# Attention in an fp32 encoder: weights times values by fp32r products of split halves for half of the key blocks, and GpSimd joins half of the two softmax maps

## The chip, the cores and the metric

The kernel runs on one core of one Trainium2 chip. The metric is the device time of one execution in microseconds. Three executions of the kernel before gave 3018.87, 3022.2 and 3027.47 us, median 3022.2 us.

## The reference

A trunk of two layers, in fp32, on two requests that share the weights: a long one of 2048 tokens ("prompt") and a short one of 256 ("sample"). The first layer is differential attention with 8 heads, the second mixes tokens with a Fourier transform. What matters here is the attention of one head:

```python
s = jnp.einsum('bhmqd,bhmkd->bhmqk', qb, k) * scale        # two maps, m = 0, 1
s = s - (slopes[:, None, None] * dist)[None, :, None]
p = jax.nn.softmax(s, axis=-1)
pd = p[:, :, 0] - lam * p[:, :, 1]
return jnp.einsum('bhqk,bhkv->bhqv', pd, v)
```

There are 16 blocks of 128 query rows and 16 blocks of 128 keys in the prompt; a value row has 128 elements. The sample has two blocks of each.

## The kernel before

The program is a sequence of stages on one core: a projection (tiles `ia_`), attention (`pa_`), an output projection (`oa_`), a gate (`fg_`), the Fourier stage (`fl_`) and a last projection (`of_`). In all but the attention's score and value products, a product of fp32 precision is already written as three fp32r products: each operand is split in a high and a low fp32r part, and high by high, low by high and high by low are added up (lines 206 to 208). Only the attention stage (`attend`) changes.

`attend` walks over 8 heads, and in each head over 17 steps `q`: 16 blocks of query rows and one step (`SAMPLE`, q = 16) for the sample. Steps overlap: in step q the scores of block q are made, block q-1 is joined, and block q-2 is transposed (`turned_block`). The order of the work within a step is written by hand in the function `step` of each engine, and each engine runs its list in order.

- **PE** makes the scores of a block in four halves of 1024 columns (`score_half`, lines 1051 to 1055; halves 0 and 1 belong to the first map, 2 and 3 to the second; one of a map's halves has a small diagonal product more, line 1054). A half goes into one of three slots (`RING`) of the PSUM tile `score`, and waits until ACT has taken the half three before it: half 1 of a step waits for exponential 2 of the step before, half 3 for exponential 0 of its own step. Between the halves stand `turn(c)`, four transpositions of 128x128 of the joined weights into the only PSUM tile `turned` (`turn_weights`, line 1083, c = 0 to 3), and `pair(n)`, two key blocks of weights times values (`pair_product`, line 1114). A product of 128x256 is for two query blocks at once, so half of the 16 key blocks come in one step (keys 0 to 7, "part 0") and the rest in the next ("part 1"). In steps 1 to 5 of a head `turn_value` also transposes the head's values.
- **ACT** copies `turned` to SBUF (`take_weights`, line 1181; `take_v`, line 1187), and computes the exponentials (line 1201). Its order is take 0, take 1, exponential 0, take 2, exponential 1, take 3, exponential 2, (values), exponential 3.
- **DVE** takes the maximum of each half (`maximum`, line 1267), turns two of them into the bias of the exponentials (`negative`, line 1273), inverts the row sums (line 1294), and joins the maps: `combine` (line 1305) computes p0 / sum0 + p1 in one instruction of 128x2048.
- **POOL** (GpSimd) scales the second map by -lambda / sum1 first (line 1358, 128x2048).

PE's order of one step before:

```python
half(0); half(1); turn(0); pair(0); turn(1); half(2); pair(1)
turn(2); half(3); turn(3); pair(2); turn_value(q - 1); pair(3)
```

Steps 6 to 15 of a head have all of this and no values to transpose; the prediction calls them, and step 0, plain steps. In step 3 `pair` has only the sample's product, in step 16 the score halves are the sample's, two and short.

## Time and profile before

| | |
|---|---|
| median of three executions | 3022.2 us (3018.87 to 3027.47) |
| the profiled execution's own time | 3030.89 us |
| its span, first to last instruction | 3029.0 us |
| TensorE clock granted, mean over the span | 0.973 |
| busy share of the span, PE / DVE / ACT / POOL | 94% / 64% / 58% / 37% |
| share of the 16 DMA engines, queue q1 | 40.1% |

The profiled execution took 8.7 us (0.3%) more than the median. The shares are means over stages of different kinds. The attention stage lasts from 817 to 2113 us of the span, eight heads of some 159 us each. Matmuls are pipelined and the ends of their rows are modelled, so the step from one start to the next says more of PE than a duration does.

### The profile page before, as it was taken

What the parts mean: (1) busy time and instruction counts of PE and PEld (TensorE: products, weight loads), DVE (VectorE), ACT (ScalarE), POOL (GpSimd) and SP (SyncE); (2) the same over time, 40 slices, a digit from 0 to 9 for tenths busy, and PEclk for the clock granted to TensorE, in tenths of its full rate; (3) what the DMA queues carried; (4) which work ended last, traced back from release to release, by engine and by line L of the source; (5) the groups of instructions that cost most, each with busy time, mean ns of one, the idle gap of its engine ahead of it and who ended that gap; (6) DMA issues with size and microseconds to landing.
All of it is one profiled execution on the core that took longest, in us unless ns stands there. A gap on an engine that the chain in (4) does not pass through costs nothing. (4 is left out here: it accounts for less than half of the span.)

```text
span 3029.0 us, 43689 instructions
## 1 busy us (share of the span) xinstructions
PE 2849.5 (94%) x15098; PEld 2495.8 (82%) x15098; DVE 1945.9 (64%) x2402; ACT 1744.5 (58%) x3126; POOL 1134.4 (37%) x676
## 2 busy tenths in 40 slices
PE   3889999999899999999999999998899899899899
PEld 3889998999878787878787878887688899887687
DVE  7668867866478787878787878787886200351322
ACT  4667766776477777767777777775443321221321
POOL 5887764654222222212222222222664221130642
PEclk8999999999999999999999999999899999999899
DMA  2555454457345414132223232021664622565752
GB/s 84 181 169 165 147 184 133 126 179 194 114 102 164 104 32 105 36 81 63 70 65 78 63 79 64 29 89 33 219 206 153 212 89 76 145 181 180 264 180 105
DMA packets 281842, 374.29 MB, mean 124 GB/s; under 512 B 22923, under 2 KB 258507, under 8 KB 276140
## 3 DMA queue, kind: packets, MB, share of 16 engines
q1 hardware_dynamic: 279404, 369.14, 40.1%
q8 instruction: 127, 2.08, 0.3%
q10 hardware_dynamic: 2080, 2.10, 0.2%
q14 instruction: 103, 0.84, 0.1%
q0 software_dynamic: 128, 0.13, 0.0%
HBM read 258.04 MB, written 125.97 MB: 127 GB/s over the span
## 5 line engine op out<-in xcount | busy, mean ns | idle before, releaser
L1267 DVE TENSOR_REDUCE pa_half_max<-pa_score 128x1 f32<-128x1024 f32 x512 | 625.7, 1222 | 234.8 <-PE pa_score L1055 233.9
L1358 POOL TENSOR_SCALAR pa_p<-pa_p,pa_inv_sum,pa_lam_neg 128x2048 f32<-128x2048 f32 x128 | 263.3, 2057 | 946.3 <-DVE pa_inv_sum L1294 946.3
L1201 ACT ACTIVATE pa_p<-pa_score,pa_neg_max 128x1024 f32<-128x1024 f32 x512 | 568.3, 1112 | 76.2 <-DVE pa_neg_max L1273 72.9
L206 PE MATMUL ia_acc<-ia_xh,ia_wh 128*128 128x384 f32 x1344 | 461.1, 343 | 82.4 <-DVE ia_xl L686 44.2
L1114 PE MATMUL pa_o_acc<-pa_wt,pa_vv 128*128 128x256 f32 x2048 | 511.4, 380 | 1.0 <-ACT pa_o_out_s L1236 0.3
L1051 PE MATMUL pa_score<-pa_ka,pa_qa 128*128 128x512 f32 x1024 | 456.7, 446 | 20.2 <-ACT pa_p L1201 9.2
L207 PE MATMUL ia_acc<-ia_xl,ia_wh 128*128 128x384 f32 x1344 | 457.2, 340 | 0.0
L208 PE MATMUL ia_acc<-ia_xh,ia_wl 128*128 128x384 f32 x1344 | 456.8, 340 | 0.0
L1181 ACT ACTIVATE pa_wt<-pa_turned 128x512 f32<-128x512 f32 x512 | 306.5, 599 | 260.8 <-PE pa_turned L1083 260.4
L1055 PE MATMUL pa_score<-pa_kb,pa_qb 96*128 96x512 f32 x1024 | 424.1, 414 | 0.0
L1114 PEld LDWEIGHTS pa_o_acc<-pa_wt,pa_vv 128*128 128x128 f32 x2048 | 367.3, 190 | 44.9 <-ACT pa_o_out_s L1236 2.1
L443 POOL TENSOR_TENSOR ia_w_sums<-ia_raw 128x512 f32<-128x512 f32 x240 | 334.7, 1402 | 178.5 <-PE ia_acc L208 156.3
L206 PEld LDWEIGHTS ia_acc<-ia_xh,ia_wh 128*128 128x128 f32 x1344 | 258.8, 193 | 89.3 <-issue 89.1
L1083 PE MATMUL pa_turned<-pa_ident,pa_p 128*128 128x128 f32 x2048 | 314.7, 276 | 10.4 <-ACT pa_wt L1181 9.6
L1083 PEld LDWEIGHTS pa_turned<-pa_ident,pa_p 128*128 128x128 f32 x2048 | 238.8, 140 | 90.6 <-ACT pa_wt L1181 49.5
L1305 DVE SCALAR_TENSOR_TENSOR pa_p<-pa_p,pa_inv_sum 128x2048 f32<-128x2048 f32 x128 | 300.3, 2346 | 0.1
L670 DVE TENSOR_TENSOR ia_wl<-ia_acc,ia_wh 128x512 fp32r<-128x512 f32 x336 | 227.7, 684 | 95.8 <-ACT ia_acc L569 94.5
L706 DVE TENSOR_TENSOR ia_c<-ia_c,ia_acc 128x384 f32<-128x384 f32 x384 | 198.6, 548 | 126.5 <-PE ia_acc L208 116.7
L207 PEld LDWEIGHTS ia_acc<-ia_xl,ia_wh 128*128 128x128 f32 x1344 | 259.0, 193 | 0.9 <-issue 0.6
L208 PEld LDWEIGHTS ia_acc<-ia_xh,ia_wl 128*128 128x128 f32 x1344 | 258.6, 192 | 0.0
L1051 PEld LDWEIGHTS pa_score<-pa_ka,pa_qa 128*128 128x128 f32 x1024 | 196.7, 192 | 65.7 <-ACT pa_p L1201 21.2
L1055 PEld LDWEIGHTS pa_score<-pa_kb,pa_qb 96*128 96x128 f32 x1024 | 197.3, 193 | 33.3
(281 smaller groups left out, 4843.4 us busy)
## 6 DMA issues: line engine op xcount, KB each, us to landing
ia_raw<-attn_w_in SPq DMA_DIRECT2D x46, 1024.0 KB, 6.7
qk_hi<-ia_hi SPq DMA_DIRECT2D x96, 192.0 KB, 3.4
qk_lo<-ia_c SPq DMA_DIRECT2D x96, 192.0 KB, 3.2
pa_ka<-qk_hi SPq DMA_DIRECT2D x32, 512.0 KB, 6.6
fl_slices<-normed SPq DMA_DIRECT2D x26, 512.0 KB, 6.6
ia_h<-x_cols SPq DMA_DIRECT2D x24, 384.0 KB, 6.4
v<-ia_c SPq DMA_DIRECT2D x48, 192.0 KB, 5.8
attn_gate<-ia_c SPq DMA_DIRECT2D x48, 192.0 KB, 1.9
```

The costliest lines, as they stand in the source:

```text
L206: pe.matmul(out, a_hi(k), b_hi(k), start=first and n == 0, stop=False)
L207: pe.matmul(out, a_hi(k), b_lo(k), start=False, stop=False)
L208: mm = pe.matmul(out, a_lo(k), b_hi(k), start=False, stop=last and n == len(ks) - 1)
L443: pool.tensor_tensor(w_sums[:, s % RING], x, y, op).then_inc(w_sum, 1)
L1051: pe.matmul(out[:, c], qa[s][:, n, at:at + P], ka[hs][:, n, cols], start=True, stop=False)
L1055: mm = pe.matmul(out[:, c], qb[s][:, n, at:at + P], kb[hs][n][:, cols], start=False, stop=True)
L1083: mm = pe.transpose(turned[:, x * P:(x + 1) * P], src, ident[:])
L1114: mm = pe.matmul(o_acc[:], vv[:, k], wt[:, g % 2, k], start=k == 0, stop=k == NB - 1)
L1181: act.activation(wt[:, s, 4 * c:4 * c + 4, at:at + P], turned[:].rearrange("p (k t) -> p k t", k=4), ACT.Copy).then_inc(turned_out, 1)
L1201: act.activation(dst[:, half * HALF:(half + 1) * HALF], score[:, (4 * q + j) % RING].rearrange("p a b -> p (a b)"), ACT.Exp, bias=neg_max[ ...
L1267: dve.tensor_reduce(half_max[:, q % 2, n, half:half + 1], score[:, (4 * q + j) % RING].rearrange("p a b -> p (a b)"), AX_X, ALU.max).then_ ...
L1305: dve.scalar_tensor_tensor(out=a, in0=a, scalar=inv_sum[:, par, 0:1], in1=p1[:, par], op0=ALU.mult, op1=ALU.add).then_inc(weights, 1)
```

## The change

Key blocks 4 to 11 (`LOW = (1, 2)`, the transposition groups c = 1 and 2) are held as two fp32r tiles each instead of one of fp32. ACT's copy of `turned` writes the high part (`wt_hi`, `vv_hi`), DVE then subtracts it from `turned` and writes the low part (`weights_low`, `v_low`). PE's product of such a block is three fp32r matmuls of 128x256 in place of the fp32 one. A transposition that follows group 1 or 2 now waits, besides for ACT's copy, for DVE's subtraction (`low_out`). In PE's order pair(2) stands ahead of turn(3), and pair(3) ahead of the values.

Joining the maps is divided: DVE's `combine` and GpSimd's first scaling cover keys 0 to 1023; for keys 1024 to 2047 GpSimd does it all, with two scalings and an addition of 128x1024 (`weights_rest`), for which turn(2) and exponential 3 wait. Tiles are laid out anew to make room: the sample's diagonal table is dropped (one DMA of 64 KB less in each head), and the lambda vectors and the squares of the tail lie where other tiles lie at other times.

```diff
     SHORT, T0 = S_SAMPLE, S_PROMPT
+    LOW = (1, 2)
+    LOW_NB = 4 * len(LOW)
     SCORES = 4 * NB + 2
...
-        vv = m.sb("vv", [P, NB + 2, P])
+        vv = m.sb("vv", [P, NB + 2 - LOW_NB, P])
+        vv_hi = m.sb("vv_hi", [P, LOW_NB, P], F32R)
+        vv_lo = m.sb("vv_lo", [P, LOW_NB, P], F32R)
-        wt = m.sb("wt", [P, 2, NB, PAIR])
+        wt = m.sb("wt", [P, 2, NB - LOW_NB, PAIR])
+        wt_hi = m.sb("wt_hi", [P, 2, LOW_NB, PAIR], F32R)
+        wt_lo = m.sb("wt_lo", [P, 2, LOW_NB, PAIR], F32R)
...
-        weights = m.sem("weights")
+        weights, weights_rest = m.sem("weights"), m.sem("weights_rest")
...
                 def turn_weights(h, t, c):
+                    b = turned_block(t)
                     if c == 0:
                         pe.wait_ge(weights, STEPS * h + t - 1)
+                    if c == 2:
+                        pe.wait_ge(weights_rest, NB * h + t - 1 if t >= 2 else NB * h)
                     wait(pe, turned_out, unit(h, t, "w", c))
-                    b = turned_block(t)
+                    wait(pe, low_out, lows(h, t, "w", c))
                     for x in range(4):
                         if b == SAMPLE:
...
                         pe.wait_ge(turned_out, unit(h, NC, "v", NC - 1) + 1)
+                        pe.wait_ge(low_out, lows(h, 1 + LOW[-1], "v", LOW[-1]) + 1)
                     for k in range(k0, k0 + 2):
-                        mm = pe.matmul(o_acc[:], vv[:, k], wt[:, g % 2, k], start=k == 0, stop=k == NB - 1)
+                        if not is_low(k):
+                            mm = pe.matmul(o_acc[:], vv[:, full_at(k)], wt[:, g % 2, full_at(k)], start=k == 0, stop=k == NB - 1)
+                            continue
+                        at = low_at(k)
+                        pe.matmul(o_acc[:], vv_hi[:, at], wt_hi[:, g % 2, at], start=False, stop=False)
+                        pe.matmul(o_acc[:], vv_hi[:, at], wt_lo[:, g % 2, at], start=False, stop=False)
+                        pe.matmul(o_acc[:], vv_lo[:, at], wt_hi[:, g % 2, at], start=False, stop=False)
                     if k0 == NB - 2:
                         mm.then_inc(pair_done, 1)
 
...
                     turn(2)
                     half(3)
+                    pair(2)
                     turn(3)
-                    pair(2)
+                    pair(3)
                     turn_value(q - 1)
-                    pair(3)
...
                     s, at = (b // 2) % 2, (b % 2) * P
-                    act.activation(wt[:, s, 4 * c:4 * c + 4, at:at + P], turned[:].rearrange("p (k t) -> p k t", k=4),
-                                   ACT.Copy).then_inc(turned_out, 1)
+                    dst = wt_hi[:, s, low_at(4 * c):low_at(4 * c) + 4, at:at + P] if c in LOW else \
+                        wt[:, s, full_at(4 * c):full_at(4 * c) + 4, at:at + P]
+                    act.activation(dst, turned[:].rearrange("p (k t) -> p k t", k=4), ACT.Copy).then_inc(turned_out, 1)
 
                 def take_v(h, t, c):
                     act.wait_ge(turns, unit(h, t, "v", c) + 1)
                     n = 4 if c < NC else 2
-                    act.activation(vv[:, 4 * c:4 * c + n], turned[:, :n * P].rearrange("p (k t) -> p k t", k=n),
-                                   ACT.Copy).then_inc(turned_out, 1)
+                    dst = vv_hi[:, low_at(4 * c):low_at(4 * c) + n] if c in LOW else vv[:, full_at(4 * c):full_at(4 * c) + n]
+                    act.activation(dst, turned[:, :n * P].rearrange("p (k t) -> p k t", k=n), ACT.Copy).then_inc(turned_out, 1)
 
...
                         act.wait_ge(weights, STEPS * h + q - (1 if q >= 2 else 2))
+                    if j == 3 and not (is_first(h) and q < 2):
+                        act.wait_ge(weights_rest, NB * h + (q - 1 if q >= 1 else -1))
...
-                    a, par = p0[:, (q - 1) % 4], (q - 1) % 2
-                    dve.scalar_tensor_tensor(out=a, in0=a, scalar=inv_sum[:, par, 0:1], in1=p1[:, par],
+                    a, par = p0[:, (q - 1) % 4, :HALF], (q - 1) % 2
+                    dve.scalar_tensor_tensor(out=a, in0=a, scalar=inv_sum[:, par, 0:1], in1=p1[:, par, :HALF],
                                              op0=ALU.mult, op1=ALU.add).then_inc(weights, 1)
+
+                def weights_low(h, t, c):
+                    dve.wait_ge(turned_out, unit(h, t, "w", c) + 1)
+                    b = turned_block(t)
+                    s, at = (b // 2) % 2, (b % 2) * P
+                    ks = slice(low_at(4 * c), low_at(4 * c) + 4)
+                    dve.tensor_tensor(wt_lo[:, s, ks, at:at + P], turned[:].rearrange("p (k t) -> p k t", k=4),
+                                      f32(wt_hi[:, s, ks, at:at + P]), ALU.subtract).then_inc(low_out, 1)
+
+                def v_low(h, t, c):
+                    dve.wait_ge(turned_out, unit(h, t, "v", c) + 1)
+                    ks = slice(low_at(4 * c), low_at(4 * c) + 4)
+                    dve.tensor_tensor(vv_lo[:, ks], turned[:].rearrange("p (k t) -> p k t", k=4),
+                                      f32(vv_hi[:, ks]), ALU.subtract).then_inc(low_out, 1)
 
                 def step(h, hs, q):
                     parts = step_parts(h, q)
+
+                    def low(c):
+                        if parts["weights"] and (q, "w", c) in place:
+                            weights_low(h, q, c)
                     if q == SAMPLE:
                         maximum_sample(h, 0)
                         inverse_sums(h, q)
                         maximum_sample(h, 1)
+                        low(1)
+                        low(2)
                     else:
                         if parts["score"]:
                             maximum(h, q, 0)
@@ -1319,11 +1381,17 @@
                         if parts["score"]:
                             maximum(h, q, 1)
                             negative(h, q, 0)
+                        low(1)
+                        if parts["score"]:
                             maximum(h, q, 2)
+                        low(2)
+                        if parts["score"]:
                             maximum(h, q, 3)
                             negative(h, q, 1)
                     if parts["before"]:
                         combine(h, q)
+                    if parts["score"] and (q, "v", q - 1) in place and q - 1 in LOW:
+                        v_low(h, q, q - 1)
                 dve.memset(ones[:], 1.0).then_inc(tail_set, 1)
                 dve.memset(eps[:], SUBLN_EPS).then_inc(tail_set, 1)
...
+                    pool.tensor_scalar(p1[:, par, HALF:], p1[:, par, HALF:], inv_sum[:, par, 1:2], lam["neg"][:, 0:1],
+                                       ALU.mult, ALU.mult).then_inc(p1_rest, 1)
+                    pool.tensor_scalar(b, b, inv_sum[:, par, 0:1], ones[:, 0:1], ALU.mult, ALU.mult).then_inc(p0_rest, 1)
+                    hold(pool, pool_rest, p1_rest, NB * h + q)
+                    hold(pool, pool_rest, p0_rest, NB * h + q)
+                    pool.tensor_tensor(b, b, p1[:, par, HALF:], ALU.add).then_inc(weights_rest, 1)
                     if is_last(h) and q == 13:
                         pool.wait_ge(unit_in, 48)
                         for n in range(2):
```

On PE, a plain step of part 0 in the attention stage, from half 2's product pair on. Before (L1114 is an fp32 product of a pair, L1083 the transpositions, L1051, L1054 and L1055 the scores):

```order
L1114 MATMUL pa_o_acc<-pa_wt,pa_vv 128x256 x2
L1083 MATMUL pa_turned<-pa_ident,pa_p 128x128 x4
L1051 MATMUL pa_score<-pa_ka,pa_qa_51 128x512
L1055 MATMUL pa_score<-pa_kb,pa_qb_52 128x512
L1051 MATMUL pa_score<-pa_ka,pa_qa_51 128x512
L1054 MATMUL pa_score<-pa_diag_53,pa_ident_r 128x128
L1055 MATMUL pa_score<-pa_kb,pa_qb_52 128x512
L1083 MATMUL pa_turned<-pa_ident,pa_p 128x128 x4
L1114 MATMUL pa_o_acc<-pa_wt,pa_vv 128x256 x4
```

Now (L1148 is the fp32 product, L1151 to L1153 the three fp32r ones, L1113 the transpositions, L1078 and L1082 the scores):

```order
L1148 MATMUL pa_o_acc<-pa_wt,pa_vv 128x256 x2
L1113 MATMUL pa_turned<-pa_ident,pa_p 128x128 x4
L1078 MATMUL pa_score<-pa_ka,pa_qa 128x512
L1082 MATMUL pa_score<-pa_kb,pa_qb 128x512
L1078 MATMUL pa_score<-pa_ka,pa_qa 128x512
L1082 MATMUL pa_score<-pa_kb,pa_qb 128x512
L1151 MATMUL pa_o_acc<-pa_wt_hi,pa_vv_hi 128x256
L1152 MATMUL pa_o_acc<-pa_wt_lo,pa_vv_hi 128x256
L1153 MATMUL pa_o_acc<-pa_wt_hi,pa_vv_lo 128x256
L1151 MATMUL pa_o_acc<-pa_wt_hi,pa_vv_hi 128x256
L1152 MATMUL pa_o_acc<-pa_wt_lo,pa_vv_hi 128x256
L1153 MATMUL pa_o_acc<-pa_wt_hi,pa_vv_lo 128x256
```

Pair(2), now six matmuls of fp32r instead of two of fp32, has moved in front of the last transpositions.

On DVE, a plain step from the first bias on. Before (L1267 maximum, L1273 bias, L1305 join):

```order
L1273 TENSOR_SCALAR pa_neg_max<-pa_half_max 128x1
L1266 REGISTER_ALU
L1267 TENSOR_REDUCE pa_half_max<-pa_score 128x1
L1266 REGISTER_ALU
L1267 TENSOR_REDUCE pa_half_max<-pa_score 128x1
L1273 TENSOR_SCALAR pa_neg_max<-pa_half_max 128x1
L1297 REGISTER_ALU
L1305 SCALAR_TENSOR_TENSOR pa_p<-pa_p,pa_inv_sum 128x2048
```

Now (L1309 maximum, L1315 bias, L1355 the low parts, L1347 join):

```order
L1315 TENSOR_SCALAR pa_neg_max<-pa_half_max 128x1
L1351 REGISTER_ALU
L1355 TENSOR_TENSOR pa_wt_lo<-pa_turned,pa_wt_hi 128x4x128
L1308 REGISTER_ALU
L1309 TENSOR_REDUCE pa_half_max<-pa_score 128x1
L1351 REGISTER_ALU
L1355 TENSOR_TENSOR pa_wt_lo<-pa_turned,pa_wt_hi 128x4x128
L1308 REGISTER_ALU
L1309 TENSOR_REDUCE pa_half_max<-pa_score 128x1
L1315 TENSOR_SCALAR pa_neg_max<-pa_half_max 128x1
L1339 REGISTER_ALU
L1347 SCALAR_TENSOR_TENSOR pa_p<-pa_p,pa_inv_sum 128x1024
```

A low part now stands ahead of the third and another ahead of the fourth maximum, and the join is half as wide.

## Rows read from the trace of the kernel before

**Rows 1.** Attention stage: us, busy PE, PEld, DVE, ACT, POOL, then clock, DMA share, GB/s.
```profile
817.00:2113.00 1296.00, 1258.38 (x6712) 1031.78 (x6712) 1031.40 (x1221) 938.01 (x1725) 280.51 (x151) 0.99 0.28 75
```

**Rows 2.** PE in order of time, a plain step: start us, duration us, instruction.
```profile
...
1543.58 0.58 PE L1051 MATMUL pa_score<-pa_ka,pa_qa 128*128 128x512 f32 x1
...
1544.71 0.39 PE L1051 MATMUL pa_score<-pa_ka,pa_qa 128*128 128x512 f32 x1
...
1545.76 0.60 PE L1083 MATMUL pa_turned<-pa_ident,pa_p 128*128 128x128 f32 x4
...
1547.06 0.64 PE L1083 MATMUL pa_turned<-pa_ident,pa_p 128*128 128x128 f32 x4
1547.45 0.48 PE L1051 MATMUL pa_score<-pa_ka,pa_qa 128*128 128x512 f32 x1
...
1548.48 1.03 PE L1114 MATMUL pa_o_acc<-pa_wt,pa_vv 128*128 128x256 f32 x4
1549.35 0.60 PE L1083 MATMUL pa_turned<-pa_ident,pa_p 128*128 128x128 f32 x4
1549.70 0.48 PE L1051 MATMUL pa_score<-pa_ka,pa_qa 128*128 128x512 f32 x1
...
1550.84 0.60 PE L1083 MATMUL pa_turned<-pa_ident,pa_p 128*128 128x128 f32 x4
1551.27 1.89 PE L1114 MATMUL pa_o_acc<-pa_wt,pa_vv 128*128 128x256 f32 x8
...
1552.82 0.58 PE L1051 MATMUL pa_score<-pa_ka,pa_qa 128*128 128x512 f32 x1
```

**Rows 3.** DVE in order of time, same step.
```profile
1551.04 1.23 DVE L1267 TENSOR_REDUCE pa_half_max<-pa_score 128x1 f32<-128x1024 f32 x1 [1.13 <-PE pa_score L1055]
1552.30 0.21 DVE L1273 TENSOR_SCALAR pa_neg_max<-pa_half_max 128x1 f32<-128x1 f32 x1
1552.43 2.34 DVE L1305 SCALAR_TENSOR_TENSOR pa_p<-pa_p,pa_inv_sum 128x2048 f32<-128x2048 f32 x1
```

**Rows 4.** ACT in order of time, same step.
```profile
1548.38 1.11 ACT L1201 ACTIVATE pa_p<-pa_score,pa_neg_max 128x1024 f32<-128x1024 f32 x1
...
1549.98 0.60 ACT L1181 ACTIVATE pa_wt<-pa_turned 128x512 f32<-128x512 f32 x1 [0.40 <-PE pa_turned L1083]
...
1552.55 1.12 ACT L1201 ACTIVATE pa_p<-pa_score,pa_neg_max 128x1024 f32<-128x1024 f32 x1 [0.38 <-DVE pa_neg_max L1273]
```

**Rows 5.** All engines in order of time, where a score half waits for ACT.
```profile
1495.72 1.12 ACT L1201 ACTIVATE pa_p<-pa_score,pa_neg_max 128x1024 f32<-128x1024 f32 x1 [0.47 <-DVE pa_neg_max L1273]
...
1496.98 0.19 PEld L1051 LDWEIGHTS pa_score<-pa_ka,pa_qa 128*128 128x128 f32 x1 [0.28 <-ACT pa_p L1201]
1496.98 0.50 PE L1051 MATMUL pa_score<-pa_ka,pa_qa 128*128 128x512 f32 x1
...
1498.08 0.65 PE L1083 MATMUL pa_turned<-pa_ident,pa_p 128*128 128x128 f32 x4
```

**Rows 6.** PE in order of time, fp32r products of 260 columns, Fourier stage.
```profile
2659.77 0.29 PE L206 MATMUL fl_ps<-fl_wc,fl_ring 128*128 128x260 f32 x1
...
2662.41 0.29 PE L207 MATMUL fl_ps<-fl_wc,fl_ring 128*128 128x260 f32 x1
```

**Rows 7.** DVE groups by line: a split's low part, two SBUF inputs beside GpSimd.
```profile
L670 DVE TENSOR_TENSOR ia_wl<-ia_acc,ia_wh 128x512 fp32r<-128x512 f32 x336 | 227.7, 684 | 95.8 <-ACT ia_acc L569 94.5
...
L1780 DVE TENSOR_TENSOR oa_wl<-oa_raw,oa_wh 128x1024 fp32r<-128x1024 f32 x4 | 11.8, 2983 | 8.7 <-ACT oa_wh L1715 8.7
```

**Rows 8.** POOL in order of time, the step's scaling of the second map.
```profile
1547.14 2.05 POOL L1358 TENSOR_SCALAR pa_p<-pa_p,pa_inv_sum,pa_lam_neg 128x2048 f32<-128x2048 f32 x1 [7.16 <-DVE pa_inv_sum L1294]
```

**Rows 9.** POOL groups by line: adding two tiles of 128x1024.
```profile
L1579 POOL TENSOR_TENSOR oa_g_more<-oa_b_more,oa_g_more 128x1024 f32<-128x1024 f32 x8 | 19.2, 2396 | 22.0 <-DVE oa_b_more L1789 22.0
```

**Rows 10.** PE in order of time, the step that scores the short request.
```profile
1455.85 0.64 PE L1083 MATMUL pa_turned<-pa_ident,pa_p 128*128 128x128 f32 x4
...
1457.23 0.66 PE L1083 MATMUL pa_turned<-pa_ident,pa_p 128*128 128x128 f32 x4 [0.75 <-ACT pa_wt L1181]
```

51 lines of the change are left out of this document (35 added, 16 removed).

## The prediction

> **What bounds the kernel now.** I read four views in this order: the busy time of the stage, one plain step engine by engine in order of time, the places where PE stands still, and the groups by line for the prices of what is new. In the attention stage PE is busy 1258 of 1296 us, DVE 1031, ACT 938, POOL 281, at 0.99 of the full clock, the 2.4 GHz level [rows 1]. So PE looks like the bound. The question is whether a shorter product shortens a step, and for that the step has to be walked through.
>
> I count from the start of turn(0), 1545.76 [rows 2]. The next one stands as far after the next half 0 (1552.82) as this one after 1543.58, 2.18 us, so at +9.24: **a plain step takes 9.24 us**. Within it turn(1) starts at +1.30, half 2 at +1.69, pair(1) at +2.72, turn(2) at +3.59, half 3 at +3.94, turn(3) at +5.08, pair(2) and pair(3) from +5.51, next half 0 at +7.06, half 1 at +8.19 [rows 2]. Three chains run beside PE, and the reader should see how little slack they have:
> - *Round trip of `turned`.* ACT begins its copy 0.63 after turn(2) starts (1549.98) and needs 0.60 [rows 4]; with 0.06 to PE that is 1.30 in all, just the distance of turn(0) and turn(1). No slack.
> - *Exponential 0 to half 3.* It starts at +2.62, behind take 1 [rows 4]. A half that waits for an exponential starts 1.26 after the exponential's start (1495.72 to 1496.98) [rows 5]. So half 3 could start at +3.88; it does at +3.94. Slack 0.06.
> - *Half 3 to the next half 1.* Half 3 gives the fourth maximum at +5.28, the bias at +6.54 [rows 3], exponential 2 at +6.79 [rows 4], half 1 possible at +8.05; it starts at +8.19. Slack 0.14.
>
> **The change, part by part.**
>
> *Products on PE.* A pair of fp32 blocks takes 0.87 (1548.48 to 1549.35) [rows 2], 0.434 per block. The nearest fp32r product is one of 260 columns, 0.120 from start to start (22 intervals in 2.64 us) [rows 6]; three make 0.36, and a low pair takes 0.71 instead of 0.87. The bounds for one product are 0.107 (256 columns at 2.4 GHz) and 0.145, at which three cost what the fp32 form does. I take 0.119. Eight heads by eight query pairs by eight low blocks are 512 blocks, so PE is spared some 0.08 x 512 = 41 us. The Trainium skill, "TensorE: Matmul & The Clock Gate", section "Back-to-back issue gap", gives N/2.4 + 2.5 ns, 109 ns for 256 columns; by it PE would be spared 54 us; the trace is 9 ns slower at 260 columns than that formula.
>
> *Low parts on DVE.* The nearest row is the same operation on the same shape, 0.684 [rows 7], and that stage's GpSimd is busy too, so I add nothing for it. DVE starts it 0.04 after ACT's end, as ACT starts after DVE's bias [rows 3, 4]; an instruction that depends on nothing starts 0.08 before the modelled end of the one ahead, as the join does [rows 3]. Two of them cost 1.37 in a step; the join of half the width gives back some 1.07 of its 2.34 [rows 3]. DVE's total is no bound (8 of 9.2 us). Their place is what matters: the second stands ahead of the fourth maximum.
>
> *A step of part 0* (pair 1 full, pairs 2 and 3 low). turn(2) at +3.59 as before; take 2 from +4.22 to +4.82; low part +4.86 to +5.55; fourth maximum at +5.47, where it was +5.28. All behind it moves by 0.19: exponential 2 at +6.98, half 1 at +8.24, while PE by itself would be there at +7.87. The next turn(0), 1.05 later, is at **+9.29**. PE's 0.32 is spent on waiting, and 0.05 more.
>
> *A step of part 1* (pairs 0 and 1 low). turn(1) stays at +1.30, since the round trip holds it: pair(0)'s 0.16 is gone. pair(1) brings turn(2) to +3.43 (its own round trip with the low part, 1.30 + 0.04 + 0.68 = 2.02 after turn(1), allows +3.32). Half 3 is then held by exponential 0 until +3.88. Half 3 and the full pair(2) (1.14 + 0.87), which stands in front now, put turn(3) at +5.89, where it was +5.08; take 3 runs from +6.52 to +7.12, and exponential 2, behind it on ACT, starts at +7.05. Half 1 at +8.31, next turn(0) at **+9.36**; PE alone would allow +9.08.
>
> *What a wait adds.* The half that waited in [rows 5] takes 1.10 without a diagonal product, where half 1 took 1.05 with it (1544.71 to 1545.76) [rows 2]: its weights cannot be loaded early. That is 0.05 and the diagonal product (128 columns at 2.4 GHz, 0.05), 0.10 in all. A wait shorter than a weight load costs less and one that disturbs what follows costs more, so the bounds are 0 and 0.16; I take 0.08. With it a plain step takes (9.29 + 9.36)/2 + 0.08 = 9.40, 0.16 more than now. Ten such steps and step 0, eight heads: 88 x 0.16 = **+14 us**.
>
> *The other steps.* In step 16 no half 2 or 3 hides the round trips, turn(2) to turn(3) is 1.38 already [rows 10], and both gain a subtraction (0.68 + 0.04 each), against which pair(2) now stands between them: +0.4 per head. In step 3 the pairs 1 to 3 are missing: two subtractions, partly hidden by the wait that half 3 has there anyway, +0.2. Steps 1, 2 and 5, in which the values' transposition makes PE's path longer than the chains, keep some 0.12 each: -0.35. Together +0.25 x 8 = **+2 us**. Bounds: nothing and +8.
>
> *Costs of nothing.* GpSimd does three scalings of half of 2.05 [rows 8] and an addition of 2.40 [rows 9], 5.5 us, instead of 2.05; it has 7.16 idle us in front of each scaling [rows 8], and turn(2) and exponential 3 want the result in the next step only. If that cover went, its excess would count in every step. The extra waits before exponential 3 and turn(2) are met long before. The dropped table of the short request is one DMA per head off a queue that nobody waits for here.
>
> The **sum** is +16 us: 3030.9 (the profiled execution, span 3029.0) becomes 3047; against the median, from which the profiled one stands 8.7 us off, **3038 us**. I call a difference under 0.3% (9 us) no change; the three executions differ by as much. Own bounds: 88 times 0.08 for the wait either way and 0.05 of reading error give 3026 to 3050.
>
> **The rivals.**
> 1. *PE's saving arrives.* The chains have more slack than the rows show, for instance because exponentials and maxima move up together when PE is earlier. A plain step becomes (8.92 + 9.08)/2 = 9.00: 88 x -0.24 = -21, with -3 from the others -24, so 2998 us; at most the 41 us. For it speaks PE's share and that each slack is a few hundredths, the precision of my reading; against it that half 1 hangs on the subtraction by a chain with no gap in it. Chance 0.28.
> 2. *A wash.* A waiting half costs nothing and the losses of steps 3 and 16 hide: 88 x 0.08 - 3 = +4, 3026 us. Chance 0.20.
> 3. *GpSimd and DVE collide.* With two SBUF inputs beside a GpSimd addition, a DVE instruction of 128x1024 took 2.98 [rows 7], where half of the join's 2.34 is 1.17. If GpSimd's addition still ran when the join starts (about +6.9), the join would end 1.8 later, some 0.9 of which the maxima could not hide: 104 steps x 0.9 = +90 us, 3115. It decides from about 1 us of overlap on. GpSimd's 5.5 us begin at +1.4 [rows 8] and end at +6.9, so they hardly meet. Chance 0.04. The Trainium skill, "GPSIMD Engine Reference", says that GpSimd shares its SBUF interfaces with VectorE and contends with DVE instructions of two SBUF inputs; by that rule the join collides and the low parts, which read PSUM and one SBUF tile, do not. The trace agrees on both (2983 ns, and 684 ns beside a busy GpSimd).
> 4. *The change doesn't spare PE anything:* a product costs 0.145, for loads that can't be hidden. Then turn(3) is late by another 0.16 in part 0 and a step takes 9.5: 3047 us. Chance 0.06.
>
> **How the numbers follow.** The forecast has 0.42. Slower by over 0.3% are it and rivals 3 and 4: 0.52; no change 0.20; faster 0.28. The likeliest case gives 3038 us; the range must reach into rival 1 on one side and past rival 4 on the other: 2992 to 3056 leaves out rival 3, the far end of rival 1 and the upper tail, less than 2 in 10. The likeliest case's own range is 3026 to 3050.
>
> **What would show it.** In the changed profile: low pairs of 0.71; low parts of 0.68; plain steps of 9.3 to 9.5, counted from one inverse of sums to the next; half 1 standing still before a weight load, released by ACT's exponential 2, which itself is released by DVE's bias (part 0) or follows take 3 at once (part 1); DVE at over 85% and PE under 93% of the stage; the join at 1.2 to 1.3 us. Wrong it is if plain steps take 9.1 or less, if half 1 never waits, or if the fourth maximum starts at half 3's end and not at the low part's.

## The result, and the profile after

| | before | after |
|---|---|---|
| median, this comparison | 3022.45 us (3018.87 to 3027.47, 4 executions) | 3039.66 us (3039.18 to 3041.48, 4) |
| ratio to before | | 1.006, 95% interval 1.0047 to 1.0072 |
| the profiled execution's own time, span | 3030.89, 3029.0 us | 3041.48, 3039.7 us |
| TensorE clock granted, mean | 0.973 | 0.971 |

The change makes the kernel 0.6% slower: 17 us by the medians, 10.6 us by the two profiled executions. The first table of the page and the attention stage, in the columns of [rows 1]:

```profile
PE 2841.4 (93%) x15610; PEld 2502.0 (82%) x15610; DVE 2003.8 (66%) x2674; ACT 1743.1 (57%) x3126; POOL 1632.3 (54%) x1060
...
817.00:2120.00 1303.00, 1247.16 (x7213) 1034.96 (x7214) 1079.95 (x1489) 936.55 (x1723) 776.25 (x534) 0.99 0.28 75
```

PE has 11 busy us less than in [rows 1] and the stage is 7 us longer or more; the clock is at the same level. Which waits end last has changed. The waits between 1100 and 2000 us of the span (engine and line waited for, us in total, times, longest), before:

```profile
DVE pa_half_max L1267 <- PE pa_score L1055: 169.7, 204, 5.4
...
PEld pa_score L1051 <- ACT pa_p L1201: 9.0, 21, 0.6
```

and after:

```profile
POOL pa_p L1427 <- DVE pa_inv_sum L1336: 319.5, 90, 8.8
...
DVE pa_wt_lo L1355 <- ACT pa_wt_hi L1222: 98.1, 169, 1.4
PEld pa_score L1078 <- ACT pa_p L1243: 31.5, 66, 0.6
DVE pa_half_max L1309 <- PE pa_score L1082: 30.0, 47, 4.8
```

Before, the maxima waited for PE 204 times, now 47 times; score halves wait for an exponential 66 times, where it was 21. PE's saving has turned into waiting. The prices of the new instructions, by groups of the same stretch:

```profile
L1435 POOL TENSOR_TENSOR pa_p<-pa_p 128x1024 f32<-128x1024 f32 x90 | 214.0, 2378 | 16.5 <-POOL pa_p L1432 16.5
...
L1347 DVE SCALAR_TENSOR_TENSOR pa_p<-pa_p,pa_inv_sum 128x1024 f32<-128x1024 f32 x90 | 133.8, 1487 | 0.7 <-issue 0.7
...
L1355 DVE TENSOR_TENSOR pa_wt_lo<-pa_turned,pa_wt_hi 128x512 fp32r<-128x512 f32 x180 | 124.5, 692 | 99.5 <-ACT pa_wt_hi L1222 98.1
...
L1427 POOL TENSOR_SCALAR pa_p<-pa_p,pa_inv_sum,pa_small 128x1024 f32<-128x1024 f32 x90 | 108.0, 1200 | 319.5 <-DVE pa_inv_sum L1336 319.5
```

A plain step of the kind that the prediction walked through (step 8 of head 4), all engines in order of time, from turn(2) of a step of part 0 to half 1 of the next. These rows answer to [rows 2 to 4]:

```profile
1544.12 0.60 PE L1113 MATMUL pa_turned<-pa_ident,pa_p 128*128 128x128 f32 x4
1544.47 0.48 PE L1078 MATMUL pa_score<-pa_ka,pa_qa 128*128 128x512 f32 x1
1544.76 0.60 ACT L1222 ACTIVATE pa_wt_hi<-pa_turned 128x512 fp32r<-128x512 f32 x1 [0.56 <-PE pa_turned L1113]
...
1544.87 2.39 POOL L1435 TENSOR_TENSOR pa_p<-pa_p 128x1024 f32<-128x1024 f32 x1 [0.18 <-POOL pa_p L1432]
...
1545.39 0.69 DVE L1355 TENSOR_TENSOR pa_wt_lo<-pa_turned,pa_wt_hi 128x512 fp32r<-128x512 f32 x1 [0.42 <-ACT pa_wt_hi L1222]
1545.60 0.28 PE L1151 MATMUL pa_o_acc<-pa_wt_hi,pa_vv_hi 128*128 128x256 f32 x1
...
1545.99 1.21 DVE L1309 TENSOR_REDUCE pa_half_max<-pa_score 128x1 f32<-128x1024 f32 x1
...
1546.33 0.60 PE L1113 MATMUL pa_turned<-pa_ident,pa_p 128*128 128x128 f32 x4
...
1547.24 0.21 DVE L1315 TENSOR_SCALAR pa_neg_max<-pa_half_max 128x1 f32<-128x1 f32 x1
...
1547.37 1.28 DVE L1347 SCALAR_TENSOR_TENSOR pa_p<-pa_p,pa_inv_sum 128x1024 f32<-128x1024 f32 x1
1547.48 0.40 PE L1078 MATMUL pa_score<-pa_ka,pa_qa 128*128 128x512 f32 x1
1547.49 1.11 ACT L1243 ACTIVATE pa_p<-pa_score,pa_neg_max 128x1024 f32<-128x1024 f32 x1
...
1548.75 0.50 PE L1078 MATMUL pa_score<-pa_ka,pa_qa 128*128 128x512 f32 x1 [0.16 <-ACT pa_p L1243]
...
1549.90 0.60 PE L1113 MATMUL pa_turned<-pa_ident,pa_p 128*128 128x128 f32 x4
```

Read it as a chain: take 2, the low part 0.63 after its start, the fourth maximum right behind the low part (1545.99, while half 3's last product started at 1545.37), the bias, exponential 2 (1547.49), and half 1, 1.26 later (1548.75). Next half 0 starts at 1547.48 and its four products would be through at about 1548.6; PE waits there. Six products of pair(2) take from 1545.60 to 1546.33, 0.73.

The next step, of part 1, counted from turn(0) at 1549.90:

```profile
1551.88 0.60 ACT L1222 ACTIVATE pa_wt_hi<-pa_turned 128x512 fp32r<-128x512 f32 x1 [0.74 <-PE pa_turned L1113]
...
1552.37 1.11 ACT L1243 ACTIVATE pa_p<-pa_score,pa_neg_max 128x1024 f32<-128x1024 f32 x1
...
1553.34 0.60 PE L1113 MATMUL pa_turned<-pa_ident,pa_p 128*128 128x128 f32 x4
...
1553.69 0.48 PE L1078 MATMUL pa_score<-pa_ka,pa_qa 128*128 128x512 f32 x1
...
1555.68 0.60 PE L1113 MATMUL pa_turned<-pa_ident,pa_p 128*128 128x128 f32 x4
...
1556.32 0.60 ACT L1222 ACTIVATE pa_wt<-pa_turned 128x512 f32<-128x512 f32 x1 [0.66 <-PE pa_turned L1113]
...
1556.82 1.11 ACT L1243 ACTIVATE pa_p<-pa_score,pa_neg_max 128x1024 f32<-128x1024 f32 x1
...
1558.07 0.19 PEld L1078 LDWEIGHTS pa_score<-pa_ka,pa_qa 128*128 128x128 f32 x1 [0.43 <-ACT pa_p L1243]
...
1559.21 0.60 PE L1113 MATMUL pa_turned<-pa_ident,pa_p 128*128 128x128 f32 x4
```

Here turn(3) is late (1555.68), take 3 with it (1556.32), and exponential 2 follows take 3 at once (1556.82); half 1 starts 1.25 after it.

**Intervals.** In each step DVE inverts the row sums once; from one inverse to the next, in us, for head 6:

| step | before | after |
|---|---|---|
| 0, 1, 2 | 9.40, 9.14, 9.47 | 9.25, 8.83, 9.81 |
| 3, 4, 5 | 9.36, 9.78, 9.71 | 9.52, 9.25, 9.37 |
| 8, 9, 10, 11 | 9.25, 9.25, 9.24, 9.23 | 9.28, 9.41, 9.28, 9.41 |
| 16 | 7.91 | 8.76 |

Over all eight heads the attention stage is 12.6 us longer, counted from the first inverse to the last: steps 6 to 15 give +5.9, step 16 +12.8, step 0 -0.6, steps 1 to 5 together -5.5. (From the last inverse to the end of the span the execution after is 2.6 us shorter, ahead of the first it is 0.7 longer; the code there is the same.) "Plain mean" below is the mean of steps 6 to 14 over all heads: before 9.285, after 9.336. In steps 6 and 7 a tail of what the values cost is still in it: from step 8 to 14 the means of head 6 are 9.24 before and 9.34 after, +0.10. The mark matters a little: from one half 0 of PE to the next a plain step of head 6 takes 9.24 before and 9.35 after, and step 16 takes 8.20 and 8.91.

### The profile page after: what moved, and what is told of

It is laid out like the page before. It is cut to its first block and busy times, and to the rows that moved or that the text cites. A ratio compares the mean times of both kernels' runs of the same rounds, so it can differ in the third digit from the quotient of the medians.

```text
span 3039.7 us, 46705 instructions
## 1 busy us (share of the span) xinstructions
PE 2841.4 (93%) x15610; PEld 2502.0 (82%) x15610; DVE 2003.8 (66%) x2674; ACT 1743.1 (57%) x3126; POOL 1632.3 (54%) x1060
## 5 line engine op out<-in xcount | busy, mean ns | idle before, releaser
L1309 DVE TENSOR_REDUCE pa_half_max<-pa_score 128x1 f32<-128x1024 f32 x512 | 623.5, 1218 | 43.2 <-PE pa_score L1082 41.9
L1078 PE MATMUL pa_score<-pa_ka,pa_qa 128*128 128x512 f32 x1024 | 453.4, 443 | 26.7 <-ACT pa_p L1243 12.3
L1082 PE MATMUL pa_score<-pa_kb,pa_qb 96*128 96x512 f32 x1024 | 423.4, 413 | 0.0
L1427 POOL TENSOR_SCALAR pa_p<-pa_p,pa_inv_sum,pa_small 128x1024 f32<-128x1024 f32 x128 | 153.6, 1200 | 457.3 <-DVE pa_inv_sum L1336 457.3
L1113 PE MATMUL pa_turned<-pa_ident,pa_p 128*128 128x128 f32 x2048 | 315.3, 276 | 22.2 <-DVE pa_wt_lo L1355 20.8
L1435 POOL TENSOR_TENSOR pa_p<-pa_p 128x1024 f32<-128x1024 f32 x128 | 304.3, 2377 | 23.5 <-POOL pa_p L1432 23.5
L1113 PEld LDWEIGHTS pa_turned<-pa_ident,pa_p 128*128 128x128 f32 x2048 | 239.1, 140 | 85.9 <-DVE pa_wt_lo L1355 21.2
L1355 DVE TENSOR_TENSOR pa_wt_lo<-pa_turned,pa_wt_hi 128x512 fp32r<-128x512 f32 x256 | 177.1, 692 | 149.1 <-ACT pa_wt_hi L1222 147.4
L1078 PEld LDWEIGHTS pa_score<-pa_ka,pa_qa 128*128 128x128 f32 x1024 | 197.0, 192 | 88.4 <-ACT pa_p L1243 52.9
L1148 PE MATMUL pa_o_acc<-pa_wt,pa_vv 128*128 128x256 f32 x1024 | 266.0, 382 | 0.2
L1222 ACT ACTIVATE pa_wt_hi<-pa_turned 128x512 fp32r<-128x512 f32 x256 | 153.2, 598 | 164.1 <-PE pa_turned L1113 164.1
L1222 ACT ACTIVATE pa_wt<-pa_turned 128x512 f32<-128x512 f32 x256 | 153.1, 598 | 156.8 <-PE pa_turned L1113 154.3
```

Source lines behind the costliest of these rows:

```text
L1078: pe.matmul(out[:, c], qa[s][:, n, at:at + P], ka[hs][:, n, cols], start=True, stop=False)
L1082: mm = pe.matmul(out[:, c], qb[s][:, n, at:at + P], kb[hs][n][:, cols], start=False, stop=True)
L1113: mm = pe.transpose(turned[:, x * P:(x + 1) * P], src, ident[:])
L1148: mm = pe.matmul(o_acc[:], vv[:, full_at(k)], wt[:, g % 2, full_at(k)], start=k == 0, stop=k == NB - 1)
L1222: act.activation(dst, turned[:].rearrange("p (k t) -> p k t", k=4), ACT.Copy).then_inc(turned_out, 1)
L1309: dve.tensor_reduce(half_max[:, q % 2, n, half:half + 1], score[:, (4 * q + j) % RING].rearrange("p a b -> p (a b)"), AX_X, ALU.max).then_ ...
```

## The experiments

Twelve kernels ran, in four comparisons of three rounds; the median of before in them was 3023.82, 3025.26, 3025.74 and 3023.66 us. Ratios are to these. Unless another base is named, the edit is made to the changed kernel.

### Are the low parts alone what takes PE's saving?

x1 leaves out DVE's 256 low parts of the weights (the tile is filled with zeros once, the products are all made) and the waits for them:

```diff
-        low_order = [x for x in order if x[2] in LOW]
+        low_order = [x for x in order if x[2] in LOW and x[1] == "v"]
...
                     def low(c):
-                        if parts["weights"] and (q, "w", c) in place:
-                            weights_low(h, q, c)
+                        return
```

> The changed kernel without DVE's low parts of the weights and without the waits for them; wt_lo is set to zero once, so the low part of the weights is left out of the sum, while PE runs the same three products. Theory (chains): the second low part no longer delays the fourth maximum, but turn(3) still stands behind pair(2), and take 3 holds exponential 2 on ACT (turn(3) +5.79 and +5.89, exponential 2 +6.95 and +7.05, next turn(0) +9.26 and +9.36 before any waiting cost). So plain steps stay at 9.25 to 9.40 and the time is 3025 to 3040 us; only step 16 gains its 0.5 us per head. Rival (the subtractions on DVE are what swallows PE's saving): plain steps fall to 9.0 to 9.1, time 3000 to 3010 us.

Measured: 3019.23 us (3014.48 to 3027.15), ratio 0.9987 (0.9976 to 0.9998), plain mean 9.302; in head 6 the steps of part 0 take 9.22 to 9.23 and those of part 1 9.40 to 9.43, step 16 takes 7.35. The time lies between the ranges of both theories: the plain steps are as expected, step 16 gave far more than the 0.5 us per head.

x2 is x1 with PE's order of before (turn(3) ahead of pair(2)):

> x1 and in addition PE's order of before: turn(3) ahead of pair(2), the values ahead of pair(3). The low part of the weights is left out of the sum. Theory: the fourth maximum and take 3 are both early again; exponential 2 at +6.79, half 1 at +8.05 to +8.15, next turn(0) at +9.10 to +9.20: plain steps 9.1 to 9.2, time 3008 to 3022 us, 10 to 20 us less than x1. That is all of PE's 41 us that the chains of the old order let through. Rival (the order is of no importance): same as x1 within 3 us.

Measured: 3013.66 us (3006.04 to 3015.19), ratio 0.9956 (0.994 to 0.9971), plain mean 9.12. Both are in the expected ranges.

What follows: without the low parts the changed kernel is 20 us faster than with them, yet by its medians 5 us (0.1%) better than before, with 41 us of PE work gone. Most of the 20 us is not in plain steps: from the first inverse to the last x1 is 16.1 us shorter than the changed kernel, and step 16 has 13.6 of it. Plain steps of part 1 stay at 9.4 without any low part, as the prediction's chain over take 3 says. With the old order they are shorter, but by 0.18 on the mean and 6 us in all, where I expected 10 to 20; in the profiled executions the stage is 9.8 us shorter, as steps 6 to 15 give 16.2, and steps 3 to 5 and 16 take 7.7 back.

### Is PE's own time of any worth?

x3 makes only the product of the high parts, so that a low block costs PE 0.12 instead of 0.36; the two other products are left out:

```diff
                         pe.matmul(o_acc[:], vv_hi[:, at], wt_hi[:, g % 2, at], start=False, stop=False)
-                        pe.matmul(o_acc[:], vv_hi[:, at], wt_lo[:, g % 2, at], start=False, stop=False)
-                        pe.matmul(o_acc[:], vv_lo[:, at], wt_hi[:, g % 2, at], start=False, stop=False)
```

> The changed kernel with one fp32r product (high by high) for a low block instead of three; the two products with low parts are left out of the sum, DVE still makes the low parts. PE is spared another 2 x 0.119 x 512 = 122 us. Theory (PE is not the bound of a plain step): plain steps stay at 9.25 to 9.40, time 3020 to 3040 us. Rival (PE is the bound, as its share of busy time says): 3039 - 122 = 2917 us.

Measured: 3034.57 us (3025.96 to 3036.83), ratio 1.0039 (1.0023 to 1.0056), plain mean 9.316. 1024 products of 0.12 us are gone, 122 us of PE's path, and the time falls by 5 (the stage by 6.3 in the profiled executions). In the profile half 1 of a step of part 0 stands where it stood, 8.22 after turn(0) (1549.91 in x3, 1540.53 in the changed kernel); the idle time in front of its weight load, 0.61 us there in the changed kernel, is now 1.22, and PE's own 0.78 where it was 0.16:

```profile
1558.13 0.19 PEld L1078 LDWEIGHTS pa_score<-pa_ka,pa_qa 128*128 128x128 f32 x1 [1.22 <-ACT pa_p L1241]
1558.13 0.50 PE L1078 MATMUL pa_score<-pa_ka,pa_qa 128*128 128x512 f32 x1 [0.78 <-ACT pa_p L1241]
```

PE with a busy share of 96% of the stage does not bound it. This run settles the case against rival 1.

### What is the new place of pair(2) worth?

x4 puts back PE's order:

```diff
                     half(3)
-                    pair(2)
                     turn(3)
-                    pair(3)
+                    pair(2)
                     turn_value(q - 1)
+                    pair(3)
```

> The changed kernel with PE's order of before (turn(3) ahead of pair(2)), nothing left out. Theory: turn(3) now waits for the second low part, +5.60 in part 0 and +5.44 in part 1 where half 3 ends at +5.08 and +5.02, and all pairs come behind it: next turn(0) +9.44 and +9.60, plain steps 9.45 to 9.6, time 3045 to 3062 us. Rival (the moved pair(2) is itself what costs, by making take 3 late): plain steps 9.2 to 9.3, time 3020 to 3032 us.

Measured: 3078.79 us (3075.81 to 3081.87), ratio 1.0184 (1.0167 to 1.0201), plain mean 9.634 (in head 6 9.55 in part 0, 9.66 in part 1). The direction is as expected, the size is beyond the range: of the 43.0 us by which the stage is longer than in the changed kernel, 20.1 lie in steps 6 to 15, and 23.3 in steps 0 to 5, which the expectation had not priced. turn(3), which stands right behind half 3 again, waits for the second low part; everything on PE behind it waits too. Over 1100 to 2000 us:

```profile
PEld pa_turned L1113 <- DVE pa_wt_lo L1355: 79.2, 91, 1.6
```

against 19.5 us in the changed kernel. The new order is what keeps the change from costing 1.8%: it saves 39 us as long as the low parts are there, and costs 6 when they are not (x1, x2). Where no values are transposed (step 0 and steps 6 to 16) it differs by the place of pair(2) alone, and there x4 is 26.5 us longer; in steps 1 to 5 pair(3) and the values change places too, and no run holds the two apart.

### The order on ACT

x7 puts exponential 2 ahead of take 3 in the steps in which no values are transposed:

> The changed kernel with one pair of instructions on ACT exchanged in the steps without values: exponential 2 ahead of take 3; nothing is left out. Theory: in part 1 (odd steps from 7 on, 9.41 to 9.44 us in the changed kernel) exponential 2 is ready at +6.83 but waits for take 3 until +7.05, so those steps shrink by 0.15 to 0.22 to 9.2 to 9.28; in part 0 (even steps, 9.28) the low part sets it, nothing changes. Time 3029 to 3035 us. Rival (take 3 is hidden and something else sets the odd steps): odd steps stay at 9.4, time 3039 us.

Measured: 3051.07 us (3049.99 to 3055.6), ratio 1.009 (1.0073 to 1.0107). Steps of part 1 fell from 9.41 to 9.22, as expected: take 3 does hold exponential 2 there. But steps of part 0, which I had expected unchanged, rose from 9.28 to 9.70, and the time lies 16 us above my range. The profile of x7 shows why, at the end of a step of part 1 and the start of the step of part 0 behind it (turn(0) at 1543.03):

```profile
1540.62 1.11 ACT L1243 ACTIVATE pa_p<-pa_score,pa_neg_max 128x1024 f32<-128x1024 f32 x1 [1.05 <-DVE pa_neg_max L1319]
...
1541.73 0.59 ACT L1222 ACTIVATE pa_wt<-pa_turned 128x512 f32<-128x512 f32 x1
...
1542.20 1.11 ACT L1243 ACTIVATE pa_p<-pa_score,pa_neg_max 128x1024 f32<-128x1024 f32 x1
...
1543.29 0.39 ACT L1275 ACTIVATE pa_o_out<-pa_o_acc 128x256 f32<-128x256 f32 x1
...
1543.73 0.73 PEld L1148 LDWEIGHTS pa_o_acc<-pa_wt,pa_vv 128*128 128x128 f32 x4 [0.35 <-ACT pa_o_out L1275]
...
1544.70 0.60 PE L1113 MATMUL pa_turned<-pa_ident,pa_p 128*128 128x128 f32 x4
```

ACT stands still for 1.05 us ahead of exponential 2 and copies `turned` only then, so exponential 3 is 0.5 late (1542.20, 1.58 behind exponential 2, where it is 1.11 in the changed kernel). Behind it ACT copies the finished sum of products (`o_out`, L1275), once in two steps, at the start of part 0. That copy now starts 0.26 after turn(0), where it started 0.21 before it, and pair(0) waits for it. So turn(1) comes at +1.67 instead of +1.30, and the rest of the step behind it: half 1 stands at +8.55 instead of +8.22. ACT's order has no free improvement there: take 3 costs nothing in the idle time in front of exponential 2.

### The divided join, alone and not at all

x5 is the changed kernel with DVE joining the whole row and GpSimd only scaling; x6 is the kernel before with the divided join and nothing else. DVE's part of x6's edit:

```diff
-                    a, par = p0[:, (q - 1) % 4], (q - 1) % 2
-                    dve.scalar_tensor_tensor(out=a, in0=a, scalar=inv_sum[:, par, 0:1], in1=p1[:, par],
+                    a, par = p0[:, (q - 1) % 4, :HALF], (q - 1) % 2
+                    dve.scalar_tensor_tensor(out=a, in0=a, scalar=inv_sum[:, par, 0:1], in1=p1[:, par, :HALF],
```

> The changed kernel without GpSimd's share of the join: DVE joins all 2048 keys in one instruction, GpSimd only scales the second map; nothing is left out. Theory: the split products need that share. The join ends some 1.07 us later, the first maximum of the next step starts at its end instead of at half 0's, the first bias and with it exponential 0 come about 0.2 us late, and half 3 hangs on exponential 0: plain steps 9.45 to 9.55 instead of 9.34, time 3048 to 3062 us. Rival (DVE has enough idle time, 83 of 100 us busy): same as the changed kernel within 4 us.

> The kernel before with GpSimd's share of the join only, fp32 products as before. Theory: DVE hangs on no chain of the old plain step, so shortening its join gives nothing there: plain steps 9.23, time 3018 to 3027 us, like before. Rival A (GpSimd's load or its contention with DVE costs something by itself): over 3030 us. Rival B (the join was part of a chain): plain steps under 9.15, time under 3015 us.

Measured: x5 3056.09 us (3050.91 to 3058.92), ratio 1.0098 (1.0081 to 1.0114), plain mean 9.45. x6 3022.61 us (3013.18 to 3028.34), ratio 0.9987 (0.9974 to 1.0001), plain steps 9.20 to 9.24. Both as expected. By itself the divided join does nothing; beside the low parts it is worth 16 us.

### One group split instead of two

x8 splits only key blocks 4 to 7 (`LOW = (1,)`), with PE's order of before; x9 is the same with the new order.

> Only key blocks 4 to 7 are split (one group, whose low part is not in front of the fourth maximum), PE's order as before, GpSimd's share of the join kept; nothing is left out. Theory: the steps of part 0 get PE's 0.32 as far as the slack of half 1 allows, 9.10 to 9.15 us; those of part 1 stay at 9.23; step 16 pays one subtraction, +0.3 us per head. Time 3012 to 3022 us, equal to before or a little less. Rival (any low part on DVE costs more than the products give): over 3030 us.

> The changed kernel with only key blocks 4 to 7 (group 1) split, but with PE's new order (pair(2) ahead of turn(3)). x8 is the same with the order of before: there steps of part 0 take 8.94 to 8.97 and steps of part 1 9.44 to 9.50. My theory, slack along the chains: without the low part of group 2 the fourth maximum stands at half 3's end again (+5.3), and with pair(2) in front turn(3) is late: in part 0 by a low pair (0.73), which take 3 can bear ahead of exponential 2 (it ends at +7.0, exponential 2 is due at +6.8), so steps of part 0 take about 9.1; in part 1 by a full pair (0.87), so they take 9.35 to 9.45. Mean 9.25, total 3022 to 3034, no better than x8. Rival, that the new order is better whatever else is changed, as it is by 39 us in the changed kernel: steps of part 0 8.8 to 8.95 and of part 1 9.2 to 9.3, total 3000 to 3015.

Measured: x8 3025.14 us (3021.46 to 3035.8), ratio 1.0005 (0.9996 to 1.0015); steps of part 0 8.94 to 8.97, of part 1 9.44 to 9.50. x9 3031.73 us (3029.1 to 3035.06), ratio 1.0022 (1.0011 to 1.0033); 9.18 to 9.21 and 9.58. x8's two kinds of steps lie further apart than expected, and its time is 3 us above my range; but the mean of its steps 8 to 14 in head 6 is 9.18, little less than the 9.24 of before, and step 16 takes the difference back (8.75 for 7.91). So its time is that of before. In x9 both kinds of steps are 0.1 longer than I expected, and 0.1 to 0.24 longer than in x8: the new order is no gain in itself. The total was in the expected range. With the old order, one group costs nothing (x8) and two cost 55 us (x4); with the new order one costs 6 us (x9) and two 17.

### The end of the stage

x10 makes GpSimd's two squares for the next stage apart, behind steps 11 and 13 of the last head, where both stand behind step 13:

```diff
-                    if is_last(h) and q == 13:
-                        pool.wait_ge(unit_in, 48)
-                        for n in range(2):
+                    if is_last(h) and q in (11, 13):
+                        if q == 11:
+                            pool.wait_ge(unit_in, 48)
+                        for n in [(q - 11) // 2]:
...
```

> The changed kernel with one edit for the end of the attention stage: GpSimd's two squares for the next stage (128x1024 each, 2.4 us), which stand together behind step 13 of the last head, are made one behind step 11 and one behind step 13. My theory: GpSimd is idle 2.7 to 3.3 us in a step, one square fits, two do not, and the interval of 11.23 us behind step 13 of the last head is their doing; it falls to 9.4 to 9.8, total 1.5 to 2 us less, 3036 to 3040 (on the same footing as the changed kernel), too little for the timing but plain in the intervals between inverses. Rival: the interval is long for the tail's DMAs or another load; then it stays at 11 or more.

Measured: 3036.06 us (3033.84 to 3040.01), ratio 1.0044 (1.0027 to 1.0061). The interval behind step 13 fell from 11.23 to 9.38, but the one behind step 11 rose from 9.47 to 10.68, and over steps 11 to 16 only 0.5 us were won. My reason, that one square fits into GpSimd's idle time, was the wrong question. In the rows of x10, GpSimd (whose addition before it ends at 2050.82) and DVE:

```profile
2050.79 1.89 POOL L1441 TENSOR_TENSOR pa_sq<-oa_b 128x1024 f32<-128x1024 f32 x1
...
2050.92 2.84 DVE L1347 SCALAR_TENSOR_TENSOR pa_p<-pa_p,pa_inv_sum 128x1024 f32<-128x1024 f32 x1
```

The join, 1.28 us in plain steps, takes 2.84 beside the square, and turn(0) waits for it. This is the mechanism of rival 3, at one place of the kernel. It asked for a test of its own.

### How near is rival 3?

x11 gives GpSimd one more pass of 128x1024 in each step, a multiplication by one, so that its addition ends 1.2 to 1.4 us later:

```diff
                     b = p0[:, (q - 1) % 4, HALF:]
+                    pool.tensor_scalar(p1[:, par, HALF:], p1[:, par, HALF:], ones[:, 0:1], ones[:, 0:1],
+                                       ALU.mult, ALU.mult).then_inc(p1_more, 1)
+                    hold(pool, more_rest, p1_more, NB * h + q)
                     pool.tensor_scalar(p1[:, par, HALF:], p1[:, par, HALF:], inv_sum[:, par, 1:2], lam["neg"][:, 0:1],
```

> The changed kernel with one more pass of GpSimd over 128x1024 (a multiplication by one, 1.20 us, 128 times) ahead of its second scaling; the output is the same. It takes away the gap that my prediction relied on: in a plain step of the changed kernel GpSimd's addition ends at 1547.24 and DVE's join of two SBUF inputs starts at 1547.37. My theory (a milder rival 3): now the addition runs some 1.1 to 1.3 us into the join, and the join takes about as much longer as the two overlap, 2.2 to 2.6 us instead of 1.28; the maxima behind it hide most of that, and a plain step takes 9.5 to 9.9 instead of 9.34, total 3055 to 3095. The theory that there is no collision in this kernel and only starts and ends matter: the join stays at 1.28 to 1.35, plain steps at 9.34, total 3038 to 3042.

Measured: 3143.85 us (3140.0 to 3148.15), ratio 1.0395 (1.037 to 1.0419), plain mean 10.19 (10.22 in head 6). So 1.2 us of GpSimd's time in a step, on an engine that idles for 3, cost 104 us. GpSimd and DVE in a plain step of x11:

```profile
1616.16 2.38 POOL L1439 TENSOR_TENSOR pa_p<-pa_p 128x1024 f32<-128x1024 f32 x1 [0.18 <-POOL pa_p L1436]
...
1616.37 3.25 DVE L1348 SCALAR_TENSOR_TENSOR pa_p<-pa_p,pa_inv_sum 128x1024 f32<-128x1024 f32 x1
1619.54 1.21 DVE L1310 TENSOR_REDUCE pa_half_max<-pa_score 128x1 f32<-128x1024 f32 x1
...
1619.86 0.63 PE L1114 MATMUL pa_turned<-pa_ident,pa_p 128*128 128x128 f32 x4 [0.67 <-DVE pa_p L1348]
```

The addition ends at 1618.54 and the join at 1619.62, 1.08 later. In x10 the square starts where the addition before it ends, and with 1.89 us of duration ends at 2052.68; the join ends at 2053.76, again 1.08 later. All 54 joins of the changed kernel that start while GpSimd's addition runs end 1.08 to 1.12 after it. So the join makes next to no progress while GpSimd runs an instruction with two inputs in SBUF, and needs 1.08 us after it. I expected 2.2 to 2.6 us and 9.5 to 9.9 per step: the direction was right, the size too small, because the join starts 0.21 us into the addition and stands still for the 2.17 us that are left of it, where I had counted on an overlap of 1.1 to 1.3. The theory that there is no collision is refuted.

The Trainium skill, "SBUF — State Buffer", section "Who interferes with whom", says that a DVE instruction with two SBUF inputs contends with a GpSimd instruction that reads SBUF. It calls the shared ports an exclusive lock; of DVE's two-port modes it says that whoever issues first gets them for the whole instruction while the other blocks fully. The joins that end 1.08 us behind GpSimd's addition agree with both.

### Step 16: waits or the collision?

x12 leaves the join of step 16 to DVE alone:

```diff
-                    a, par = p0[:, (q - 1) % 4, :HALF], (q - 1) % 2
+                    w = S if q == NB else HALF
+                    a, par = p0[:, (q - 1) % 4, :w], (q - 1) % 2
...
```

> The changed kernel, in which DVE alone joins the whole row (128x2048) in step 16 of each head and GpSimd only scales the second map there. In the changed kernel the join of 128x1024 in that step takes 2.56 us, as it starts 0.9 us after GpSimd's addition; the whole row alone takes 2.34 in the kernel before. Theory A: step 16 is long (8.76 against 7.91) because the four transpositions wait for subtractions; then the join matters little and step 16 stays at 8.5 to 8.8, total 3037 to 3041. Theory B: it is long because of the collision; then it falls to 7.9 to 8.3, total 3034 to 3037. x6 (the join divided, no subtractions) had 8.34 and x1 (no subtractions, join divided) 7.35, so they do not agree on it; I expect theory A.

Measured: 3036.12 us (3033.8 to 3039.56), ratio 1.0043 (1.0031 to 1.0056); step 16 takes 8.75 in head 6, as in the changed kernel (8.76). By the time alone theory B would do as well (3034 to 3037), but its step 16 of 7.9 to 8.3 did not come. Theory A stands: it is the waits for the subtractions. The changed kernel's rows of step 16:

```profile
1779.53 0.60 PE L1113 MATMUL pa_turned<-pa_ident,pa_p 128*128 128x128 f32 x4
...
1781.54 0.66 PE L1113 MATMUL pa_turned<-pa_ident,pa_p 128*128 128x128 f32 x4 [0.55 <-DVE pa_wt_lo L1355]
...
1782.58 2.37 POOL L1435 TENSOR_TENSOR pa_p<-pa_p 128x1024 f32<-128x1024 f32 x1 [0.18 <-POOL pa_p L1432]
...
1783.47 2.56 DVE L1347 SCALAR_TENSOR_TENSOR pa_p<-pa_p,pa_inv_sum 128x1024 f32<-128x1024 f32 x1
...
1783.61 0.66 PE L1113 MATMUL pa_turned<-pa_ident,pa_p 128*128 128x128 f32 x4 [0.69 <-DVE pa_wt_lo L1355]
```

The join collides there as well (addition to 1784.95, join to 1786.03, 1.08 later), but 2.56 us is only 0.22 more than the whole row alone (2.34), so nothing is lost by it. x12 and x10 came out 3.5 us under the changed kernel by their medians, though their attention stages are only 0.3 and 0.8 us shorter. Stages with the same code vary by more: in x12's profiled execution the first inverse came 7.9 us earlier, and the part behind the last took 3.8 us longer. Differences of 3 or 4 us between comparisons of this kernel are not read here.

## Why the prediction was right, and where it wasn't

The forecast was 3038 us, slower by more than 0.3%; measured are 3039.66 us and 1.006 (1.0047 to 1.0072). The time agrees better than the parts of it do, and that is partly luck: the sum of +16 us stands against +12.6 us in the stage, +10.6 between the profiled executions and +17 between the medians, and inside it two errors cancel.

**The plain step: right step by step.** Counted from turn(0) of the step of part 0 in the rows above, at 1540.53, take 2 starts at +4.23 (predicted +4.22), the low part at +4.86 (+4.86), the fourth maximum at +5.46 (+5.47), exponential 2 at +6.96 (+6.98), half 1 at +8.22 (+8.24). Next turn(0) is at +9.37, 1.15 behind half 1, where 1.05 with nothing waiting plus 0.08 for the wait had been predicted. PE's saving of 0.32 is spent on waiting, by the chain that the prediction named.

**A step of part 1: right chain, one price off.** The next turn(0) is at 1559.21, 9.31 later, where 9.36 + 0.08 was predicted. The late turn(3) and take 3, with exponential 2 right behind, are as predicted, each about 0.1 earlier. One statement of that walk failed: "Exponential 0 starts at +2.62, behind take 1", and with it "Half 3 is then held by exponential 0 until +3.88". Before, exponential 0 starts 0.64 behind take 1's start (1547.74) and 0.04 behind the end of the first bias (1548.13 to 1548.34, then 1548.38), and take 1 happens to end at 1548.34 too. With the shorter join the bias comes earlier (at +1.48, where it was at +2.37), and exponential 0 starts 0.49 behind take 1's start, at +2.47. That would let half 3 go at +3.73. It starts at +3.79, 0.35 behind turn(2) and with no wait in front of it, as before: nothing holds it. x7 confirms the rest of the chain by moving take 3 away: 9.22.

**The sum of the plain steps: too high.** Predicted were 88 x 0.16 = +14 us; measured are +5.9 in steps 6 to 15 and -0.6 in step 0. In steps 8 to 14 of head 6 the price is +0.10 for +0.16 (+0.13 over all heads, with a step 13 of 11.23 in the last). But it was multiplied by steps that do not follow the pattern: step 0 and step 6 became shorter (9.25 for 9.40, 9.35 for 9.66 in head 6), and step 7 stayed as it was.

**The other steps: mis-sized on both sides.** Step 16 was priced at +0.4 per head. In five ordinary heads it is +0.88 on the mean (8.94, 8.74, 8.74, 8.74, 8.76 against 7.85, 7.95, 7.91, 7.92, 7.91), and the rest of the +12.8 comes from the two heads behind which the program's loop goes back (+2.2 and +3.4) and the last head (+2.8, 7.50 for 4.73). x1 shows that the subtractions are the cause of the last and of the ordinary ones (step 16 at 7.35, the last at 4.71), x12 that the join is not. From half 0 to half 0 of PE it is +0.70 (8.21 to 8.90). In the step shown above turn(2) comes 2.01 behind turn(1), where it was 1.35, and turn(3) 2.07 behind turn(2), where it was 1.38: both subtractions are paid nearly in full, 1.35 us, and turn(1) is 0.18 late besides. pair(2) in front of turn(3) gives back 0.83; the +0.4 supposes some 1.0. For the loop's ends x1 has 11.5 in both heads against 11.3 and 9.8 before, and 13.6 and 13.2 in the changed kernel; the growth is in a wait of PE marked "issue", and its cause stays open. Steps 1, 2 and 5 were given -0.35 together, and have -0.31 in head 6 (-0.31, +0.34, -0.34), but not 0.12 less each; step 3 was given +0.2 and has +0.16. Step 4 gave -0.53 and had no term at all; no run shows why. Together the other steps were to bring +2 us and brought +7. Two errors of 9 us and 5 us with opposite signs left the sum of the stage at +12.6 where +16 was predicted. By x1 the stage without subtractions is 3.5 us shorter than before: the subtractions cost 16.1 us (3.7 of it at the loop's ends), and that is what makes the kernel slower.

**Costs of nothing.** GpSimd's chain starts at +0.60 and ends at +6.73 in the step above, 0.11 us ahead of the join. I had counted 5.5 us ending at +6.9 from a start at +1.4; it is 6.1 us long (three scalings of 1.20, not half of 2.05, an addition of 2.38 and 0.18 of waiting for itself), but starts earlier. So "they hardly meet" was right by 0.11 us, and that is luck more than a reading: its start was off by 0.8 and its length by 0.6, and the two nearly cancel. x11 shows the price when they do meet: +104 us over the changed kernel, where rival 3 had +90 over the kernel before. In steps 16 and 1 to 5 of a head they do meet; the join's mean of 1.49 (group L1347) against 1.28 comes from there. In step 16 that costs nothing (x12); for steps 1 to 5 no run shows it.

**What would show it.** Low pairs of 0.73, low parts of 0.69, the join at 1.28, half 1 released by exponential 2 and the fourth maximum behind the low part: as said or within 0.02. Two signs failed: DVE's share of the stage is 83%, not over 85, and PE's is 96%, not under 93. PE's busy time fell by 11 us instead of 41. The rows of an fp32r product are modelled at 0.28 us while the next starts 0.12 later, so busy time is no measure of what was spared; the intervals between starts are.

**The rivals.** Rival 1 is refuted by x3: with 122 us more of PE's path gone the time falls by 5. Rival 2, no change, is refuted by the interval of the ratio; its claim that a waiting half costs nothing fails by the 0.10 between 1.15 and 1.05. Rival 4 fails by the spacing of 0.12 (1545.60 to 1546.33 in six).

No complete version that was tried beats the kernel before: x6 (0.9987, to 1.0001) and x8 (1.0005) equal it. x1 and x2 are faster but leave the low parts out.

## What to carry to other kernels

A busy share of 97% does not make an engine the bound: walk one step from each wait to its releaser and write down the slack of every chain beside it. If the slacks are hundredths of a microsecond, work taken off the busy engine comes back as waiting, and new instructions on another engine's chain can cost more than was spared. Here 256 subtractions of 0.69 us cost 16 us, 13.6 of that in the short steps, where little stands between two dependent round trips. When an instruction is added to such a chain, look what can be moved in front of the wait: here the new order of PE was worth 39 us. And where GpSimd and DVE both read two tiles in SBUF, leave a gap between them and say how large it is.

## What the runs showed that I had not expected

- The join of two SBUF tiles of 128x1024 takes 1.28 us alone, and ends 1.08 us after GpSimd's two-input instruction if that runs when the join starts: 2.56, 2.84 and 3.25 us in the rows above. One more pass of 1.20 us on GpSimd made the plain steps 0.85 us longer on the mean.
- GpSimd's scaling takes 1.20 us for 128x1024 and 2.06 for 128x2048 on the mean (rows L1427 here and L1358 in [rows 8]): two halves cost 0.34 more than the whole.
- Removing 122 us of matmuls (x3) moved the time by 5 us, while PE's order in one step (x4) moved it by 39.
